# Two small copies ahead of a split, a scaling in four parts, and four copies ahead of a squaring, in the second block of a two-block transformer kernel

## The reference

```
proj = rms(x) @ w_in
qkv_a = silu(causal_conv(proj[..., :1536]))        # q_a, k_a l2-normalised; z_a follows
beta = sigmoid(proj[..., B]);  g = -exp(a_log) * softplus(proj[..., A] + dt_bias)
o_a = gated_delta_rule(q_a, k_a, v_a, g, beta)     # 4 heads, chunks of 64
o_a = rms(o_a) * silu(z_a)
q_b, k_b = rms(...), rms(...)                      # 8 heads of 64, per-head rms
o_b = stick_breaking(q_b, k_b, v_b) * silu(z_b)
merged = gate_a * (o_a @ w_up_a) + gate_b * (o_b @ w_up_b)
out = x + merged @ w_out
```

## Time and profile before

| | before |
|---|---|
| median of 3 runs | 1445.28 us (1444.82 to 1448.46) |
| the profiled execution, its own time | 1442.53 us |
| its span in the trace | 1440.8 us |
| mean granted clock of PE in it | 0.972 of full |
| PE busy | 1322.6 us (92%) |
| DVE busy | 660.4 us (46%) |
| ACT busy | 496.3 us (34%) |

### The profile page before, as it was taken

The page is one execution under the profiler, slowest core; times in us unless marked ns, Lnnn a source line. Parts: engine busy times, 40 slices in busy tenths (PEclk is TensorE's granted clock), DMA queues, the critical chain, the costliest instruction groups (busy, mean ns, idle before and its releaser), DMA issues.

```text
span 1440.8 us, 16806 instructions
## 1 busy us (share of the span) xinstructions
PE 1322.6 (92%) x7035; PEld 1016.0 (71%) x7035; DVE 660.4 (46%) x1097; ACT 496.3 (34%) x776; POOL 59.4 (4%) x70
## 2 busy tenths in 40 slices
PE   6999999999999996788887889989989988899998
PEld 5888887678766885545554468777968875488887
DVE  4455334655466445211111168657566455413253
ACT  4334234456355423011111145354232135422231
POOL 0000000000000000112111100000000001000000
PEclk9999999999999997699999999999999999899999
DMA  6222322112222368899999952102010020112331
GB/s 226 87 86 87 117 66 81 59 59 88 88 88 88 121 239 324 345 403 403 407 401 409 371 200 88 59 0 89 1 59 1 30 88 1 59 59 88 116 117 59
DMA packets 67558, 207.41 MB, mean 144 GB/s; under 512 B 9003, under 2 KB 10141, under 8 KB 55190
## 3 DMA queue, kind: packets, MB, share of 16 engines
q1 hardware_dynamic: 61234, 192.11, 35.5%
q0 software_dynamic: 5536, 12.04, 2.8%
q10 hardware_dynamic: 708, 2.13, 0.4%
HBM read 196.33 MB, written 17.83 MB: 149 GB/s over the span
## 4 chain that ended last, share of the span: by engine, by line
PE 69%; DVE 11%; DMA 10%; ACT 6%; issue 3%; POOL 1%; SPq 0%; ACTq 0%; DVEq 0%; POOLq 0%
PE PS L543 17%; PE PS L545 16%; PE PS L544 16%; PE PS L1019 5%; DMA work<-xn_scratch,slot_tokens 4%; PE PS L540 4%; PE PS L862 3%; DMA raw<-in_w 2%; DMA scratch<-in_w 2%; PE PS L890 2%; DVE wlo L1295 2%; ACT scratch L2198 2%; ACT whi L2198 1%; ACT work L2198 1%; PE PS L707 1%
## 5 line engine op out<-in xcount | busy, mean ns | idle before, releaser
L1295 DVE TENSOR_TENSOR wlo<-raw,whi 128x2048 fp32r<-128x2048 f32 x70 | 160.3, 2291 | 270.3 <-ACT whi L2198 270.2
L2198 ACT ACTIVATE whi<-raw 128x2048 fp32r<-128x2048 f32 (+1 forms) x78 | 138.7, 1779 | 235.1 <-PE PS L545 218.4
L543 PE MATMUL PS<-whi,hthi 128*128 128x512 f32 x480 | 195.6, 407 | 5.9 <-ACT y_plain L2198 4.1
L543 PE MATMUL PS<-hthi,whi 128*128 128x512 f32 x480 | 196.6, 410 | 0.9 <-DVE htlo L1338 0.9
L545 PE MATMUL PS<-whi,htlo 128*128 128x512 f32 x480 | 188.0, 392 | 0.0
L545 PE MATMUL PS<-hthi,wlo 128*128 128x512 f32 x480 | 187.8, 391 | 0.0
L544 PE MATMUL PS<-wlo,hthi 128*128 128x512 f32 x480 | 187.7, 391 | 0.0
L544 PE MATMUL PS<-htlo,whi 128*128 128x512 f32 x480 | 187.3, 390 | 0.0
L2198 ACT ACTIVATE work<-PS 128x512 f32<-128x512 f32 (+3 forms) x148 | 81.5, 563 | 304.3 <-PE PS L890 74.2
L543 PEld LDWEIGHTS PS<-hthi,whi 128*128 128x128 f32 x480 | 90.5, 188 | 32.3 <-issue 14.2
L543 PEld LDWEIGHTS PS<-whi,hthi 128*128 128x128 f32 x480 | 90.8, 189 | 24.3 <-ACT y_plain L2198 4.3
(11 more groups left out here) (357 smaller groups left out, 1843.7 us busy)
## 6 DMA issues: line engine op xcount, KB each, us to landing
raw<-in_w_in SPq DMA_DIRECT2D x44, 1024.0 KB, 5.0
y_plain<-in_w SPq DMA_DIRECT2D x21, 1024.0 KB, 26.1
w_plain<-in_w SPq DMA_DIRECT2D x20, 1024.0 KB, 20.3
h_plain<-in_w SPq DMA_DIRECT2D x20, 1024.0 KB, 23.5
raw<-in_w SPq DMA_DIRECT2D x15, 1024.0 KB, 19.4
merged<-in_w SPq DMA_DIRECT2D x10, 1024.0 KB, 26.8
scratch<-in_w SPq DMA_DIRECT2D x10, 1024.0 KB, 27.8
raw<-in_w_gate SPq DMA_DIRECT2D x8, 1024.0 KB, 5.1
```

The source lines that it names most:

```text
L543: e.matmul(o, lh, rh, start=start, stop=False)
L1295: tt(lo, raw_place(j), as_f32(hi), SUB).then_inc(*ve.mark("lo", j))
L2198: return e.activation(o, i, f, bias=bias, scale=scale)
```

## The change

One `split()` on DVE moves from ahead of the two small copies to behind the addition that uses them. The scaling of the queries becomes four instructions of 128x512, with a step of the chains after each; the number of steps stays the same. ACT copies the turned queries out before it squares the output instead of after it. Nothing else changes: the same values are computed, PE's list is the same, and so is SP's.

```diff
@@ vector, ahead of the softplus
-        split()
         on.wait_ge(*pe["dta"])
         e.tensor_copy(dta, inside("dta")[:, 0:2 * DH]).then_inc(*ve.mark("out", "dta"))
...
         tt(gl, ba[:, :, DH:], dta[:, 0:DH].unsqueeze(1).broadcast_to([P, NT, DH]), ADD).then_inc(*ve.mark("gl raw"))
+        split()
         on.wait_ge(*ac["softplus"])
@@ vector, beside_steps
                 on.wait_ge(*ac["out", name, 0, HB - 1])
-                tt(d, d, bc(r, [P, 32, SBD]), MUL).then_inc(*ve.mark(name, 0, "normed"))
-                for _ in range(PAUSE - 1):
-                    yield
+                if name == "qb":
+                    for c in range(HB):
+                        of = slice(c * SBH, c * SBH + SBH)
+                        tt(d[:, of, :], d[:, of, :], bc(r[:, of], [P, SBH, SBD]), MUL).then_inc(
+                            *ve.mark(name, 0, "normed", c))
+                        yield
+                    ve.also(name, 0, "normed")
+                else:
+                    tt(d, d, bc(r, [P, 32, SBD]), MUL).then_inc(*ve.mark(name, 0, "normed"))
+                    for _ in range(PAUSE - 1):
+                        yield
@@ scalar, after the chains
         on.wait_ge(*ve["chains"])
+        turn_block("qb", 0, qS.rearrange("p c n -> p (c n)"), gq8["q2"], [ve["chains"]])
         act(tiles(sq_out), O, ACT.Square).then_inc(*ac.mark("o squares"))
-        turn_block("qb", 0, qS.rearrange("p c n -> p (c n)"), gq8["q2"], [ve["chains"]])
```

## The result

The changed kernel takes 1433.85 us (median of 4 runs, 1433.20 to 1437.01), the kernel before, timed beside it, 1445.05 us: 11.2 us less, ratio 0.993 with a 95% interval of 0.9917 to 0.9943. Forecast were 1439.2 us and 6.1 us less, with a range of 1437.0 to 1443.0. So the direction was right, and the gain was nearly twice what was forecast and outside the range. The profiled execution of the changed kernel took 1437.01 us, span 1435.3, the slowest of its four. Trace against trace the gain is 5.5 us (1442.53 against 1437.01).

A forecast was written before the change was run, and what follows sets the result against it. PE, busy 92% of the span, was taken as the bound, so only edits where PE waits count. Terms 2.6 + 1.55 + 1.95 = 6.1 us took the median from 1445.3 to 1439.2 us, range 1437.0 to 1443.0.

The forecast's parts named there:

- Part one: Small copies and addition ahead of DVE's split: softplus's Abs and all behind it come earlier, 2.6 us less, bounds 2.0 to 2.8.
- the slack: PE's 1.12 us of idle time ahead of the chains, from which a low clock after the decays could be paid.
- PE's new idle time: Before the decays PE, waiting 1.65 us for DVE, would wait some 3.5 us and its clock probably fall.
- Part two: Scaling of the queries in four instructions: the chain's next step starts earlier, 1.55 us less, bounds 0.65 to 2.0.
- The cover ahead of `vn`: In the other chain, DVE finishes `vn` just ahead of PE's products, 0.2 us to spare; without it part two gives 0.65.
- Part three: Turned queries' copies ahead of ACT's squaring: PE starts sooner after the chains, 1.95 us less, bounds 1.8 to 2.1.
- the upper bound of the prediction: At the first stick products, DVE's clearing of two banks limits part three's gain to at most 2.1 us.
- Its measure for the clock: After the chains: 1.65 us of PE idle time left the clock up, 3.10 let it fall; 2.2 us lies between.
- The sum: Whole kernel: 2.6 + 1.55 + 1.95 = 6.1 us less, nothing behind the three places giving time back.
- pay-back at the decays: Rival: part one's gain is lost to a low clock at the decays or a late load; 1441.8 us, chance 0.14.
- delay by `vn`: Rival: the scaling's parts delay the other chain, so only 0.65 us passes on; 1440.1 us, chance 0.10.
- loss of the clock over the second half of `zb`: Slower rival: PE loses its clock at the decays and runs 14.2 us of work at half clock; 1452 us, chance 0.05.

The follow-up runs named there:

- e13: The kernel before, unchanged, profiled a second time: 1442.58 us.
- e14: The kernel before, unchanged, profiled a third time: 1442.70 us.
- e16: The changed kernel with all three edits, a fourth profile: 1435.08 us.
- e5: The kernel before plus 12 spare products in PE's idle gap ahead of the last round of stick products: 1441.34 us, ratio 0.9985.
- e6: The changed kernel plus 12 spare products in PE's idle gap ahead of the last round of stick products: 1434.93 us, ratio 0.9939.
- e9: The kernel before plus three spare products on PE ahead of the first stick products, where PE never waits: 1442.95 us, ratio 0.9996.
- e1: The kernel before with only the two small copies and the addition moved ahead of the split: 1443.54 us, ratio 0.999.
- e7: The kernel before with the copies ahead of the split and the turned copies ahead of the squares, scaling unsplit: 1437.49 us, ratio 0.9961.
- e8: The kernel before with the scaling in four parts and the turned copies ahead of the squares, split unmoved: 1439.63 us, ratio 0.9971.
- e2: The kernel before with only the scaling of the queries in four parts: 1443.90 us, ratio 0.9991.
- e15: The changed kernel with all three edits, a third profile: 1433.44 us.
- e11: The changed kernel plus eight spare products on PE ahead of the first stick products, where PE never waits: 1438.29 us, ratio 0.9957.
- e4: The changed kernel with all three edits, timed again on another chip than its first timing: 1434.32 us, ratio 0.9926.

## Why the prediction was wrong in its size

- **Part one, 2.6 forecast.** Stretch I went from 74.0 to 74.3 us in three traces to 71.1 to 71.2 in four: 3.0 us, of which up to 0.3 us is the low clock behind the decays that e13 and e14 have and the first trace before has not. The gain of Abs was taken at 2.8 and was 3.03, and the low clock after the decays came, as expected, and took only the slack. Against the prediction's reading, `bat` was not there long before: DVE could copy it only at 940.98, 1.7 us ahead of the split, which was enough. PE's new idle time was put at 3.5 us before the decays and was split, 1.16 at a bank of `za` and 1.92 there; the clock fell after the shorter one too. The rule of the Trainium skill ("TensorE: Matmul & The Clock Gate", section "The HAM clock gate (the "warmup" mystery)") agrees as far as it goes: behind this idle time the clock was low (0.50 in the window from 972.3). Had its whole penalty lain in the open, part one would by the prediction's sum have given 1.1 us; the slack covered it.
- **Part two, 1.55 forecast.** Stretch II: 1.5 us in every trace of the changed kernel. The cover ahead of `vn`, put at 0.2 us, held and was 0.3 us.
- **Part three, 1.95 forecast.** 1.81 us to the first stick products. The clock fell behind the shorter wait of 2.27 us in three of four traces of the changed kernel (0.54 in the window 1159.8 to 1163.5 of the first) and stayed up in one, e16. There the gain was 1.90 us, 0.1 more, since PE waited for the cleared banks. So the upper bound of the prediction held. Its measure for the clock, between 1.65 us of idle time that leave it up and 3.10 that let it fall, did not: in e13 and e14 it fell behind 1.54 and 1.60 us.
- **The sum, 6.1 forecast.** The three stretches give 3.0 + 1.5 + 2.0 = 6.5 us when the clock falls at the end of III in both kernels, and 9.3 us when it stays up in the changed one. The step that failed is the sentence behind the sum: that behind the three places everything hangs on what moved; the sum has no term for the clock behind them, and no rival is faster than the range. The order and the waits stay, but not the speed. In three of four traces of the changed kernel the clock no longer falls in PE's last idle stretch among the stick products, and the four products and the others behind them run at 2.4 GHz: 2.7 us (131.49 against 128.78 us), a term that was missing. That the fall costs this much, and that the timed gain beyond the three places hangs on it in good part, is shown by filling the idle stretch (e5, e6). Why the changed kernel escapes the fall is not shown. The shift of some 6 us is a likely reason: e9 shifts the same work by 0.7 us and escapes it too. But that is one trace; e1, e7 and e8 have the idle stretch 2.7 to 3.5 us earlier against the start of I and have the fall; and the changed kernel has it in one trace of four with the same shift as in the other three (6.2 us). I had looked at the clock only where the edits are.
- **From the trace to the median.** The prediction put the median 2.75 us above its sum, since the profiled execution of before lies that far below its median. The changed kernel's median of 1433.85 us lies only 0.4 to 0.6 us above two of its traces (1433.22 and 1433.44) and below the other two (1435.08 and 1437.01). These some 2 us are the rest of the miss; their cause stays open.
- **The rivals.** No pay-back at the decays, no delay by `vn`, no loss of the clock over the second half of `zb`. Of the slower rival the clock was the right suspect, at the wrong place and with the wrong sign.
- **What stays open.** The kernel before's three traces are of executions of 1442.5 to 1442.7 us, below its medians of 1443.9 to 1445.1. Of the timed gain of 10 to 11 us, 9.3 are located; some 1 to 2 us are not. Part of the scatter is ahead of the change: the last unit of `za` is split at 926.7 to 930.4 us in the traces, in kernels that are the same up to there. Why the parts alone give only 1.3 (e1) and 0.9 us (e2) where I and II show 2.7 and 1.6 is shown for e2 (stretch III, 1.2 us longer in its trace) and not for e1, whose runs range from 1438.6 to 1448.5 us.

## What to carry to other kernels

The clock behind PE's idle stretches can change between two kernels tens of microseconds away from the edit, and here that was worth 2.7 us, about as much as the largest of the three edits. Sum the edits, then list PE's idle stretches downstream (here the clock fell behind stretches of 1.4 us and more, and not each time), with the granted clock behind each, and put what the clock takes there into the range in both directions. One profile of a kernel does not tell whether such a fall is its habit; take three or four. When parts do not add up in timed runs, cut the traces into stretches at instructions that all variants share: the stretches that no edit touches show where the rest went.

## What the hardware showed that I had not expected

- The clock is not a matter of the idle time alone: PE idled 3.42 us and the clock fell (before), 3.23 us and it stayed (e9, e15), 3.29 us and it fell (the changed kernel's first profile), 1.92 us and it fell, 2.27 us and it fell or stayed (e16), 1.54 us and it fell (e13), 1.65 us and it stayed (before).
- A kernel with 0.7 us of needless work added (e9) had its stretch shortened by 2.3 us, and 1.8 us of it (e11) cost 4.0 us by the medians, against e4 on another chip, and 5.7 us in the stretch.
- The fall at the end of the stick products is repeatable in the kernel before: in three profiles its stretch III took 133.51, 133.51 and 133.49 us.
